# A feed-forward stage with its weight units taken in pairs, by seven products of halves instead of eight

## What is computed

```python
xn = modulate(rmsnorm(h, norm2_g[l]), sh2, sc2)
ff = jnp.square(jax.nn.relu(xn @ w_ff1[l])) @ w_ff2[l]      # 1024 -> 4096 -> 1024
h = h + g2[:, None, :] * ff
return rmsnorm(h, final_g)
```

## Time and profile before

| | us |
|---|---|
| median of 3 runs | 2643.6 |
| lowest and highest | 2637.7, 2644.45 |
| span of the profiled execution, first to last instruction | 2637.4 |

### The profile page before, as it was taken

How to read it: one execution, slowest core, us unless ns; L and a number is a source line. 1 busy time by engine, 2 the same in 40 slices (tenths; PEclk the granted TensorE clock), 3 DMA queues, 4 the chain that set the end, 5 groups by cost and what they waited for, 6 DMA issues and landing times.

```text
span 2637.4 us, 36451 instructions
## 1 busy us (share of the span) xinstructions
PE 2534.9 (96%) x14788; PEld 2064.3 (78%) x14788; DVE 1481.4 (56%) x2440; ACT 1028.0 (39%) x1817; POOL 300.6 (11%) x213
## 2 busy tenths in 40 slices
PE   8889999999999999999899999999999999999998
PEld 6678898999998877766577777878866687788886
DVE  4987654654445457476647787455734634433444
ACT  4465454543223253245642223354333433322323
POOL 0143210012222010000012222020000000000001
PEclk9999999999999999999999999999999999999999
DMA  4211122232323341520035663332221123232232
GB/s 171 90 49 50 56 65 65 81 89 88 96 89 93 93 143 49 175 73 2 1 116 196 195 198 126 96 104 88 87 66 48 58 94 95 81 95 92 94 96 72
DMA packets 76980, 244.83 MB, mean 93 GB/s; under 512 B 12708, under 2 KB 18213, under 8 KB 76558
## 3 DMA queue, kind: packets, MB, share of 16 engines
q1 hardware_dynamic: 69470, 215.72, 26.3%
q10 hardware_dynamic: 7344, 26.77, 3.0%
HBM read 238.25 MB, written 6.90 MB: 93 GB/s over the span
## 4 chain that ended last, share of the span: by engine, by line
PE 78%; DVE 11%; ACT 5%; issue 3%; POOL 2%; DMA 0%; SPq 0%; ACTq 0%; DVEq 0%; POOLq 0%
PE ps L590 56%; PE ps L2057 8%; DVE wl L379 2%; ACT wh L367 2%; PE ps L2784 2%; PE ps L2584 1%; PE ps L3493 1%; PE ps L1805 1%; DVE xl L671 1%; PE ps L1833 1%; DVE arena L1059 1%; PE ps L1822 1%; DVE arena L3163 1%; PE ps L2428 1%; PE ps L764 1%
## 5 line engine op out<-in xcount | busy, mean ns | idle before, releaser
L590 PE MATMUL ps<-xh,wh 128*128 128x512 f32 (+1 forms) x2728 | 1006.5, 383 | 22.7 <-DVE xl L671 7.5
L590 PE MATMUL ps<-xl,wh 128*128 128x512 f32 (+1 forms) x2728 | 988.5, 377 | 0.0
L590 PE MATMUL ps<-xh,wl 128*128 128x512 f32 (+1 forms) x2728 | 984.4, 375 | 0.0
L379 DVE TENSOR_TENSOR wl<-ring,wh 128x1024 fp32r<-128x1024 f32 x374 | 472.7, 1264 | 588.5 <-ACT wh L367 587.6
L367 ACT ACTIVATE wh<-ring 128x1024 fp32r<-128x1024 f32 x372 | 393.2, 1057 | 934.3 <-PE ps L590 838.3
L590 PEld LDWEIGHTS ps<-xh,wh 128*128 128x128 f32 x2728 | 500.1, 189 | 151.0 <-issue 41.4
L590 PEld LDWEIGHTS ps<-xh,wl 128*128 128x128 f32 x2728 | 499.7, 189 | 97.6
L590 PEld LDWEIGHTS ps<-xl,wh 128*128 128x128 f32 x2728 | 498.2, 189 | 97.7 <-issue 5.5
L2057 PE MATMUL ps<-xh,wh 128*128 128x264 f32 (+1 forms) x816 | 254.1, 311 | 5.3 <-DVE xl L433 3.8
L754 POOL TENSOR_TENSOR arena<-arena 128x512 f32<-128x512 f32 (+1 forms) x35 | 60.2, 1725 | 1610.9 <-ACT arena L739 1610.9
L2057 PE MATMUL ps<-xl,wh 128*128 128x264 f32 (+1 forms) x816 | 233.3, 286 | 0.0
(11 more groups left out here) (389 smaller groups left out, 2546.7 us busy)
## 6 DMA issues: line engine op xcount, KB each, us to landing
ring<-in_weights SPq DMA_DIRECT2D x374, 512.0 KB, 3.6
arena<-in_w_ada ACTq DMA_DIRECT2D x48, 512.0 KB, 4.6
arena<-in_cmp_w SPq DMA_DIRECT2D x2, 2048.0 KB
strip_copies<-strip_scratch SPq DMA_DIRECT2D x8, 327.5 KB, 6.9
arena<-strip_copies SPq DMA_DIRECT2D x8, 264.0 KB, 4.1
out_features<-arena SPq DMA_DIRECT2D x8, 256.0 KB, 2.1
token_scratch<-arena SPq DMA_DIRECT2D x3, 512.0 KB, 6.3
arena<-token_scratch SPq DMA_DIRECT2D x12, 128.0 KB, 3.9
```

Of the source, the lines that this page charges most:

```text
L379: dve.tensor_tensor(flat(self.wl[:, s % 2]), flat(self.ring[:, s % RING]), flat(self.wh[:, s % 2]).bitcast(F32), ALU.subtract).then_inc(se ...
L590: last = pe.matmul(self.place(u, e), w[:, k, :], x[:, k, o:o + m], start=(k == 0 and i == 0), stop=(k == self.chunks - 1 and i == 2))
```

## The change

In the third block's feed-forward, two consecutive weight units are taken as one matrix of 256 output features by 1024 input features, and cut in four quadrants (a11, a12 from the first unit, a21, a22 from the second; each 4 chunks of 128 features). The inputs are cut likewise (4 chunks by 256 tokens each). The pair's output is then made by seven products of such halves (12 matmuls of 128x256 each, 84 in all) where it took eight (48 matmuls of 128x512). The products want sums of quadrants of both sides:

- of the weights, four sums for each pair, S1 to S4, made by POOL from the ring (512 elements for each partition each), then split by ACT and DVE;
- of the inputs, four sums for each line (`Quadrants`, 1024 elements each), made by POOL, then split by ACT and DVE.

Of the unit pair's own weights only 1.5 units are split. The partial results are added up partly in PSUM, partly on DVE, in places of 256 tokens; in the first line ACT copies them out of PSUM, DVE adds the others and squares. Products 4 and 3 of a pair are put into the next pair, or behind the fourth chunk of the unit after the last pair. In the first line 11 pairs (units 6 to 27), in each line of the second 2 pairs (units 2 to 5): 19 pairs. `Normed` now keeps its eight chunks, and POOL adds the shift to each in place (128x512, one scalar) for `Quadrants`. `hidden` is written by relu and squared in place. The feed-forward's lines use three PSUM banks in place of four, the products the banks 3 to 7. Some semaphores of earlier stages get other names, since they are shared. The diff, cut to its core:

```diff
+SEVEN = 1.79
+PRODUCT = SEVEN / 7
 class Core: load_unit
+        if u - RING in self.summed:
+            sp.wait_ge(*self.summed[u - RING])
 class Line
+    def start(self, u):
+        if u <= self.pair0 or not self.pairs:
+            return u * self.d
+        t = (self.pair0 + self.pairs * SEVEN + u - self.pair1) * self.d
+        return t - 2 * PRODUCT * self.d if u == self.pair1 else t
...
+class Quadrants(Stage):
+    def __init__(self, core, at, x, ready, hi, lo, tmp, free=None, opened=None, split=(0.75, 0.66)):
+        self.begin, self.every = at + split[0], split[1]
+    def pool(self, pool):
+        yield self.at
+        self.ready(pool)
+        if self.opened:
+            pool.wait_ge(*self.opened)
+        x, t = self.x, self.tmp
+        left, right = x[:, 0:HC], x[:, HC:NC]
+        for n, (a, b) in enumerate(((left[:, :, HALF:], left[:, :, 0:HALF]), (right[:, :, HALF:], t[0]),
+                                    (right[:, :, HALF:], left[:, :, HALF:]), (right[:, :, 0:HALF], t[1]))):
+            yield self.at + 0.6 * n
+            if n % 2:
+                pool.wait_ge(self.made.sem, self.made.at((n + 1) // 2))
+            if n >= 2 and len(t) == 2:
+                pool.wait_ge(self.made.sem, self.made.at(n))
+                pool.wait_ge(self.low.sem, self.low.at(n - 1))
+            pool.tensor_tensor(t[n % len(t)], a, b, ALU.subtract).then_inc(self.made.sem, 1)
+    def scalar(self, act):      # four hi, at begin + every * n, each waits for made and for the old ones' last product
+    def vector(self, dve):      # four lo, at begin + every * n + 0.23
...
+class Sevens(Stage):
+    A, B, C = (4, 5), (3,), (6, 7)
+    def multiply(self, pe, of, p):
+        ...
+        pe.wait_ge(*split)
+        if p == 0 and ready:
+            pe.wait_ge(*ready)
+        bank = {1: self.A, 2: self.B, 5: self.C}
+        if of in bank:
+            ...
+        else:
+            pe.wait_ge(*self.read({6: 1, 7: 6, 4: 7, 3: 5}[of], p))
+        for k in range(HC):
+            for i, (w, x) in enumerate(((wh, xh), (wh, xl), (wl, xh))):
+                last = pe.matmul(self.place(of, p), w[:, k, :], x[:, k, :], ...)
+    def products(self, pe, p):
+        for n, (of, before) in enumerate(((1, 0), (2, 0), (4, 1), (6, 0), (3, 1), (5, 0), (7, 0))):
+            yield self.begin(p) + n * PRODUCT * self.line.d
+            if p >= before:
+                self.multiply(pe, of, p - before)
+    def pool(self, pool):
+        for p in range(self.n):
+            ...
+            for i, (out, a, b, op) in enumerate(((s1, a21, a22, ALU.add), (s2, s1, a11, ALU.subtract), (s3, a11, a21, ALU.subtract),
+                                                 (s4, a12, s2, ALU.subtract))):
+                yield t + (-3.2 + 1.27 * i) * d
+                ...
+                if p:
+                    pool.wait_ge(self.low.sem, self.low.at(4 * (p - 1) + i + 1))
+                pool.tensor_tensor(out, a, b, op).then_inc(self.made.sem, 1)
+    def plan(self):             # order of the splits on ACT; DVE's are half a product later
+        d = self.line.d * PRODUCT
+        for p in range(self.n + 1):
+            t = self.begin(p)
+            if p == 0:
+                yield t - 4 * d, "first", p
+            if p < self.n:
+                yield t - 0.7 * d, 0, p
+                yield t + 0.3 * d, 1, p
+                yield t + 1.7 * d, 2, p
+                yield t + 3.2 * d, "half", p
+                if p < self.n - 1:
+                    yield t + 3.6 * d, "first", p + 1
+                else:
+                    yield t + 3.6 * d, "next", 0
+                yield t + 5.2 * d, 3, p
+        yield self.line.at + self.line.start(self.line.pair1) + 0.5 * self.line.d + 2 * d, "next", 1
+class SevensSquared(Sevens):    # ACT copies 1, 6, 7, 4 out of PSUM; DVE adds 2, 5, 3 and squares two tiles for each pair
+class SevensAdded(Sevens):
+    def collect(self, dve):     # every product of a pair, 128x256, in this order (order() goes by products())
+        before = {2: 1, 3: 6, 5: 7}
+        for t, of, p in self.order():
+            yield t + 0.08 * self.line.d * PRODUCT
+            ...
+                ins = dve.scalar_tensor_tensor(out=out, in0=self.place(of, p), scalar=self.line.scale[u], in1=out, op0=ALU.mult, op1=ALU.add)
...
 class Normed
+    def pool(self, pool):
+        for k in range(NC if self.kept is not None else 0):
+            yield self.at + 0.28 * (k + 2) + 0.2
+            pool.wait_ge(self.lo.sem, self.lo.at(k + 1))
+            pool.tensor_scalar(self.out[k], self.out[k], self.shifts[k], None, ALU.add).then_inc(self.shifted.sem, 1)
 def third_block
+    up = Squared(core, 4 * NC, at, three, inputs_2, hidden, (6, 11))
+    of_norm = Quadrants(core, at + 1.6, inputs_2.kept, inputs_2.ready, hi, lo, quarters(3 * NC * T, 4))
+    pairs = SevensSquared(up, of_norm, spare_hi, spare_lo, of_weights)
+    def quadrants(g, line, inputs, ready, at):
+        x = hidden[:, g:g + NC]
+        tmp = quarters((g - NC) * T, 4) if g else early
+        opened = (read[-1].lo.sem, read[-1].lo.at(NC)) if g else (seven[-1].low.sem, seven[-1].low.at(4 * seven[-1].n))
+        t = Quadrants(core, at - 3.58, x, lambda eng: ready(eng, NC - 1), hi, lo, tmp, seven[-1].quadrants_free(), opened, (1.2, 0.4) if g else (0.75, 0.66))
+        seven.append(SevensAdded(line, t, spare_hi, spare_lo, of_weights, seven[-1], g == 0))
```

More of the change, by code:

```diff
@@ L480, in weave, with woven @@
             ahead.append((t, n, p))
+def woven(*programs):
+    ahead = [(t, n, p) for n, p in enumerate(programs) for t in [next(p, None)] if t is not None]
+    while ahead:
+        first = min(ahead, key=lambda a: a[:2])
+        ahead.remove(first)
+        t, n, p = first
+        yield t
+        t = next(p, None)
+        if t is not None:
+            ahead.append((t, n, p))
 def run(core, stages):
@@ L553, in walk @@
             yield from [(1, k) for k in chunks[NC // 2:]]
-        yield from [(u, k) for u in range(2 if both else 0, self.n) for k in chunks]
+        yield from [(u, k) for u in range(2 if both else 0, self.n) for k in chunks if not self.paired(u)]
     def planned_end(self, u):
-        return self.at + (u + 1) * self.d + (0.5 if self.alone is not None and u == 0 else 0)
+        return self.at + self.start(u + 1) + (0.5 if self.alone is not None and u == 0 else 0)
     def place(self, u, e=0):
@@ new lines, with __init__, read, tile_signal @@
+class SevensAdded(Sevens):
+    def __init__(self, line, quadrants, spare_hi, spare_lo, sums, prior=None, shared=False):
+        super().__init__(line, quadrants, spare_hi, spare_lo, sums, prior, shared)
+        self.added = self.core.take("products_added", 7 * self.n)
+        self.count = {(of, p): (self.added.sem, self.added.at(k + 1)) for k, (_, of, p) in enumerate(self.order())}
+        line.claim()
+    def read(self, of, p):
+        return self.count[of, p]
+    def tile_signal(self, u):
+        p, e = divmod(u - self.line.pair0, 2)
+        return self.count[4 if e else 3, p]
+    def collect(self, dve):
+        before = {2: 1, 3: 6, 5: 7}
+        for t, of, p in self.order():
+            yield t + 0.08 * self.line.d * PRODUCT
+            e, half = {1: (0, 0), 2: (0, 0), 6: (0, 1), 3: (0, 1), 7: (1, 1), 5: (1, 1), 4: (1, 0)}[of]
+            u = self.line.pair0 + 2 * p + e
+            out = self.line.tiles[u][:, half * HALF:(half + 1) * HALF]
+            dve.wait_ge(*self.done(of, p))
+            if of == 7:
+                dve.wait_ge(*self.count[5, p])
+            elif of in (2, 3):
+                dve.wait_ge(*self.count[before[of], p])
+            if self.line.scale is None:
+                ins = dve.tensor_tensor(out, self.place(of, p), out, ALU.add)
+            else:
+                ins = dve.scalar_tensor_tensor(out=out, in0=self.place(of, p), scalar=self.line.scale[u], in1=out, op0=ALU.mult, op1=ALU.add)
+            ins.then_inc(self.added.sem, 1)
@@ L723, in end @@
     def end(self):
[L724 removed]
+        return self.at + self.ends[-1]
     def total(self):
@@ L956, in down @@
         inputs = Inputs(core, [hidden[:, g + k] for k in range(m)], at - last.d, SEQ, ready=ready)
-        before = Added(core, at, WHOLE, banks, inputs, m, tiles, scale)
+        before = Added(core, at, WHOLE, banks, inputs, m, tiles, scale, pairs)
         stages += [inputs, before]
-        at += NC * before.d
+        if pairs[1]:
+            stages += quadrants(g, before, inputs, ready, at)
+        at += before.start(NC)
     return stages, before, at
```

375 lines of the change are left out of this document (326 added, 49 removed).

## The result

The changed kernel takes 2664.5 us (median of 4 runs, 2663.1 to 2672.7) against 2641.8 for the kernel before, measured beside it (4 runs). The ratio is 1.0096, 95% interval [1.0079, 1.0114]: slower by about 23 us, outside the range I gave. The profiled span grew from 2637.4 to 2661.7.

What follows compares the result with a forecast made beforehand. PE was taken to bound the kernel; -20.3 (matmuls) + 0.5 (first line's pairs) + 2.7 (entry) + 12.6 (second pairs) + 1.0 (last line) = -3.5 us, giving 2640 us, range 2626 to 2651.

Steps and rivals of the forecast that it cites:

- 128x512 ... I take 119.6: PE's matmuls: 119.6 ns for one of 256 columns, 1.07 us less a pair, -20.3 us for 19 pairs.
- DVE and POOL stand in each other's way: SBUF reads: a lock held for the whole instruction, DVE 0.54 to 1.08 us, POOL 1.15 for one S, 2.3 a quadrant.
- Sum 4.2 us ... met in the three lines: +12.6: Second pair of three second-line lines: PE waits before products 6, 7 and unit 6 behind POOL's quadrants, 4.2 us each.
- What is queued behind on DVE (... `Inputs`) has over 10 us of slack until the next line and costs PE nothing more: Second line, DVE's last adds, quadrants' low parts and `Inputs` behind the quadrants: over 10 us of slack, no cost to PE.
- rival (c): PE's small waits drop the clock to 1.2 GHz, 1.7 us each, up to four times: 2647; chance 0.05.
- I take +0.5 (0 to +3): First line's pairs: lock taken 9.6 of 10.05 us, up to 10.5 in strict turns, mostly absorbed by slack; +0.5 us.
- +2.7: First line's entry: POOL's shifts stretch DVE's time for an input chunk to 1.82 us, PE ends 2.7 us later.
- Rival (b): Pairs themselves bound by the lock, deciding from 10.65 us a pair; at 11.3 us the time is 2664; chance 0.14.
- Rival (a): DVE and POOL's turns cost PE little: 2627.5 to 2631.5 us, at best 2625; chance 0.34.
- Rival (d): The narrower matmuls run by the skill page's figure, 2 us less than the forecast; chance 0.05.

Runs made afterwards that it cites:

- no_reads: The changed kernel with every POOL instruction of the pairs made a memset that writes without reading; 2622.6 us, ratio 0.9934 to the kernel before.
- half_quads: late_sums with each of POOL's quadrant additions (1024 elements) cut in two of 512; 2641.2 us, ratio 0.9996 to the kernel before.
- dve_quads: late_sums with the quadrants' additions on DVE instead of POOL; 2636.3 us, ratio 0.9983 to the kernel before.
- late_sums: The changed kernel, with POOL's first-pair weight sums in the second line's four lines waiting for the line's last input; 2650.6 us, ratio 1.0044 to before.

## Why the prediction was wrong

- "128x512 ... I take 119.6": right, 119.3.
- "DVE and POOL stand in each other's way": right. no_reads shows it, by DVE's durations and by the whole loss. One reading beside it was off: the squares are 0.684 us long and not 0.75, so they hold some 0.1 us less for a pair.
- "Sum 4.2 us ... met in the three lines: +12.6": right, 4.2 in each, before products 6 and 7 and unit 6 (1.3, 1.3 and 1.4, the rest in small steps). half_quads and dve_quads show the cause. The hold of a quadrant fits what was taken, 2.3: POOL's addition of 1024 elements takes 2.41 us free.
- "What is queued behind on DVE (... `Inputs`) has over 10 us of slack until the next line and costs PE nothing more": **this step failed.** I looked at what the quadrants delay, and not at what POOL does next. POOL's first-pair S start as soon as the weights' slots are full, which is at a line's start; there `Inputs` has no slack, each chunk is read by PE as it is made. DVE's two-input splits come 1.7 us apart instead of 0.6, and PE waits four times. The forecast had 0 for these starts; they cost 13.2 us in the three further lines and 5.3 at the start of the second line, which I had put at 0 too because I looked only at its quadrants there. late_sums gives back 16.3 of these 18.5. Of the second line's start 3.4 us ran at the lower clock level (granted 0.5, 1.2 GHz, from 2450.5 to 2453.9) behind PE's waits there, the one place at which rival (c) came about, for about the 1.7 us that it named.
- The first line's units 2 to 5 were not costed at all: +5.4. POOL's quadrants and the first pair's S take their turns there while PE uses a unit each 5.57 us. The waits before units 3 and 4 (3.3 us) come from the quadrants, since they are gone in half_quads and dve_quads, and the one before unit 5 (1.7) from the S. The shift is over before them. The size of the turn was known from the same paragraph (2.3 us and DVE's own); I didn't carry it to the neighbouring stretch.
- "I take +0.5 (0 to +3)" for the first line's pairs: mis-sized, 4.7. Where both have work, the turns are strict; a pair is 10.69 us on DVE (I had "up to 10.5"), and the slack of some 2.7 us is used up before the 11 pairs are: seven of them take 0.67 us more each.
- "+2.7" at the entry: 1.6. POOL's eight shifts come 14.46/8 = 1.81 us apart, as worked out (1.82), but not for the reason given: by itself such an instruction takes 1.56 us and not 0.62, and costs DVE 0.43. And the sum counted 1.82 for all seven distances of DVE's low parts, though the text before it excepts the last two chunks: they were 1.33, 1.68, four times 1.76 and 0.92, 11.0 us in place of 12.7.
- Rival (b) gave 2664 and 2664.5 was measured. Its mechanism came about in part: seven pairs of the first line are bound by DVE, at 10.69 us, just over the 10.65 from which it was to decide. But it had 23.8 us for a loss in all 19 pairs, and the first line's eleven lost 4.7; most of the 44.6 us lies in other places. The number agrees by chance. Rival (a) is out: the waits cost 44.6 us, not the 4 to 8 of its sum.
- Rival (d), the page's figure for a matmul: at 119.3 ns the row stays 10 ns above the 109 ns of the Trainium skill (TensorE: Matmul & The Clock Gate, Back-to-back issue gap).

The mechanism was named and priced rightly at the place where I looked for it. The sum was wrong because two of the places at which it acts, the line starts and the units behind the entry, were not costed.

## What to carry to other kernels

When work goes to POOL that reads SBUF, list every stretch in which it can run, not when it is planned: an instruction whose inputs are ready early runs early, and meets whatever DVE does then. Make it wait until DVE has nothing that PE needs soon, cut it into shorter instructions, or give it to DVE. When work goes to a free engine, cost the place in its queue too: two of the three places tried for the squares on ACT lost more than they gained, by what stood behind them.

## What the runs showed of the hardware

- Where both have two-input work waiting, DVE and POOL take strict turns: DVE's instructions are back to back and POOL still gets one in between each two (1.7 us from split to split, for a split of 0.685 us and an addition of 1.29). At the entry, where POOL's shifts read one tensor, only one of DVE's two instructions for a chunk got longer, 1.18 us in place of 0.75. Neither engine's busy share shows this: both read as busy while they wait.
- The Trainium skill (SBUF — State Buffer, Who interferes with whom) names the pairs that exclude each other, and no_reads agrees: splits of 685 and 1222 ns beside POOL's writes, means of 1246 and 1738 where it reads. DVE's additions of a 256-wide product from PSUM, with one SBUF tensor, take 477 ns in the changed kernel and 482 in no_reads.
- A `tensor_scalar` of 128x512 on POOL with a column of scalars took 1.56 us free, against 0.62 at least for those of the earlier trace rows; a memset of 128x1024 took 0.96 us, the addition 2.41.
